# First MLP of a two-layer trunk: the relu's transpose moved from TensorE to VectorE and ScalarE, modulation loads issued two weight transfers later

## The chip, the cores and the metric

The kernel runs on one core of a Trainium2 chip. The metric is the device time of one launch in microseconds (us). A core has TensorE (PE, matrix products; PEld is its loading of the stationary operand), VectorE (DVE), ScalarE (ACT), GpSimd (POOL), and SyncE (SP), whose queue issues nearly all DMA transfers here. Each engine runs its own instructions in order and waits for the others through semaphores. SBUF is the on-chip memory of 128 partitions, PSUM the smaller one into which TensorE writes.

## What is computed

Two layers, each a token mixer and an MLP, with a modulation (adaLN) in front of each and a LayerNorm behind it. There are 256 tokens, `D_MODEL = 2048`, `D_FF = 8192`, all float32.

```python
mod = (c_act @ w_ada[i] + b_ada[i])[:, None, :]
sh_a, sc_a, g_a, sh_m, sc_m, g_m = jnp.split(mod, N_MOD, axis=-1)
h = x * (1.0 + sc_a) + sh_a
y = diff_attention(h, ...)            # layer 0; layer 1: sliding_window_attention
x = layer_norm(ALPHA * x + (1.0 + g_a) * y, ln_mix_g[i], ln_mix_b[i])
h = x * (1.0 + sc_m) + sh_m
y = jnp.square(jax.nn.relu(h @ w_up[i])) @ w_down[i]
x = layer_norm(ALPHA * x + (1.0 + g_m) * y, ln_mlp_g[i], ln_mlp_b[i])
```

## The kernel before

**Blocks, subtiles, quarters.** All weight products are cut into 89 blocks of 2048 x 512 weights (4 MB). A block is 8 subtiles n = 0 to 7 of 256 rows of weights; two subtiles are a weight quarter, one DMA transfer of 1 MB into `raw` (5 slots). For float32 accuracy each factor is split in a high and a low part: ScalarE makes `w_hi` from `raw` (`split_hi`, L528, 6 slots), VectorE makes `w_lo = raw - w_hi` in the place of `raw` (`split_lo`, L901), and TensorE does three products for each pair (hi x hi, lo x hi, hi x lo; L1709 to L1711): 12 matmuls of 128x512 for a subtile, 96 for a block. ScalarE may be at most 6 subtiles ahead of TensorE (semaphore `used`), and a weight quarter is loaded when TensorE has finished the quarter five before it (`load_raw`, L397). TensorE needs `w_lo` of subtile n before it can start subtile n.

**An MLP** is 32 blocks, in four rounds of 8: four up blocks (512 columns of `h @ w_up` each), then four down blocks that take the 2048 new features through `w_down`. While TensorE runs the next block b, the result of an up block is finished inside the others' order of work: ScalarE takes the relu out of PSUM (`up_relu`, L553, in `R`), the 256 x 512 result is transposed so that features lie on the partitions, ScalarE squares it twice (`SQ`, and rounded as `f_hi`), VectorE makes `f_lo = SQ - f_hi`. The up results are handled in block b with b % 8 = 0 to 3, where b counts the 31 blocks after the first of the MLP; blocks with b % 8 = 3 to 6 are the down blocks, and the first of them wants the last `f_lo` at its subtile 6.

**The transpose** is done in two ways. In the first MLP (layer 0) TensorE does it: 8 transposes (L1603, `turn_up`) behind its subtile 1 into the PSUM tile `turn[:, 0]`, which ScalarE squares (L560, L561, `up_square`, behind its subtile 4); VectorE's `f_lo` (L1031, `up_lo`) stands behind its subtile 4. In the second MLP (layer 1, `ON_CHIP = (1,)`) VectorE does it with 16 transposes of 32x256 (L1040), 8 behind subtile 2 and 8 behind subtile 3, each of which puts a 32-partition quarter of `R` into another 32-partition quarter of `RR`; ScalarE squares `RR` behind its subtile 5 (L572, L573).

**The modulation.** The product with `w_ada` is done on VectorE: a piece of 128x1024 (512 KB, `ada_w`, 4 slots) is multiplied by a column of `c` and added to `acc` (`ada_tile`, L929, first of 16: L926). `MLP_ADA` and `ADA_A` say behind which subtiles of a block VectorE takes a piece: in the first MLP 6 or 7 a block in blocks 0 to 27 (192 in all), in the second 32 in all. After every 16 pieces TensorE turns or sums `acc` (L1627, L1638) and VectorE takes the result (L960 and L961, or L987) behind its subtile 6. In blocks 0 to 3 of each MLP VectorE also does two passes over `x` behind subtile 7 (`affine`, L1311, L1312).

**SyncE's order** is written out by hand. `load_block` issues the four weight quarters of a block and, behind each, the pieces that VectorE takes in that quarter's subtiles. A piece (`load_ada`, L374) waits until VectorE has used the piece four before it, and everything behind it in the queue waits too.

## Time and profile before

| | |
|---|---|
| median of 3 runs | 2228.6 us (2226.92 to 2228.74) |
| the profiled execution | 2228.67 us, of which the span from first to last instruction is 2226.9 us |
| TensorE busy | 2168.5 us (97%) |
| VectorE busy | 1790.6 us (80%) |
| ScalarE busy | 981.3 us (44%) |
| bytes moved | 596.4 MB, 268 GB/s on average |
| granted TensorE clock | 0.993 on average, 1.00 in both MLPs |

The first MLP runs from 523.9 to about 1205 us, the second from 1520 to about 2195 us. The layer-0 attention with its projections stands from about 135 to 524 us. "Idle before" in a row is the time its engine stood still just before the instruction, and behind the arrow stands what it waited for. On VectorE and ScalarE an instruction's duration can be longer than the step to the next one's start, because neighbours may overlap.

### The profile page before, as it was taken

How to read it: one execution, taken by the hardware profiler on the slowest of the kernel's cores; microseconds unless marked ns; L12 is line 12 of the kernel's file. 1: busy time of each engine (PE TensorE's matmuls, PEld its weight loads, DVE VectorE, ACT ScalarE, POOL GpSimd, SP SyncE). 2: the span in 40 equal slices, each digit the busy share in tenths (PEclk: the TensorE clock that was granted, in tenths of full speed). 3: DMA queues.
4: the chain of work that ended last, by engine and by line, in shares of the span. 5: the costliest groups of instructions: out<-in, count | busy, mean ns of one | idle time of the engine just before them, and what ended most of it. 6: DMA issues, size and time to landing. Idle time of an engine off the chain costs nothing.

```text
span 2226.9 us, 26022 instructions
## 1 busy us (share of the span) xinstructions
PE 2168.5 (97%) x9952; PEld 1791.8 (80%) x9952; DVE 1790.6 (80%) x2057; ACT 981.3 (44%) x1330; POOL 33.4 (2%) x53
## 2 busy tenths in 40 slices
PE   6999999999999999999999999999999999999997
PEld 6887888877888888888888788777888888888886
DVE  6899998887997897888786888777966865874877
ACT  1135444546433443443353655536534443443441
POOL 0001000000000000000000000000000000000000
PEclk9899999999999999999999999999999999999999
DMA  9999888877999999999985643365766676666663
GB/s 360 384 331 347 322 320 300 306 245 256 361 364 325 354 366 335 325 380 350 323 311 190 198 152 119 122 207 190 236 221 223 213 241 206 219 217 219 228 234 113
DMA packets 262592, 596.41 MB, mean 268 GB/s; under 512 B 13426, under 2 KB 14788, under 8 KB 262468
## 3 DMA queue, kind: packets, MB, share of 16 engines
q1 hardware_dynamic: 254800, 579.45, 74.2%
q10 hardware_dynamic: 7668, 15.30, 2.2%
q8 instruction: 79, 1.29, 0.2%
q14 instruction: 45, 0.37, 0.0%
HBM read 592.60 MB, written 2.10 MB: 267 GB/s over the span
## 4 chain that ended last, share of the span: by engine, by line
PE 88%; DVE 7%; DMA 1%; issue 1%; ACT 1%; SPq 0%; DVEq 0%; POOL 0%; ACTq 0%; POOLq 0%
PE pair L1709 25%; PE pair L1711 25%; PE pair L1710 25%; DVE acc L916 2%; DVE w_lo L901 1%; PE pair L1967 1%; PE pair L1969 1%; PE pair L1968 1%; PE pair L1729 1%; PE pair L1731 1%; PE pair L1730 1%; PE turn L2041 1%; DMA y<-in_w_ada_dram 1%; PE turn L2022 1%; PE turn L1603 1%
## 5 line engine op out<-in xcount | busy, mean ns | idle before, releaser
L528 ACT ACTIVATE w_hi<-raw 128x1024 fp32r<-128x1024 f32 x712 | 726.8, 1056 | 620.2 <-PE pair L1711 297.4
L901 DVE TENSOR_TENSOR w_lo<-raw,w_hi 128x1024 fp32r<-128x1024 f32 x712 | 852.5, 1220 | 117.0 <-ACT w_hi L528 110.8
L1709 PE MATMUL pair<-w_hi,h_hi 128*128 128x512 f32 x1456 | 581.3, 399 | 1.5 <-DVE w_lo L901 0.8
L1711 PE MATMUL pair<-w_hi,h_lo 128*128 128x512 f32 x1456 | 567.8, 390 | 0.0
L1710 PE MATMUL pair<-w_lo,h_hi 128*128 128x512 f32 x1456 | 567.3, 390 | 0.0
L1709 PE MATMUL pair<-w_hi,f_hi 128*128 128x512 f32 x1056 | 414.0, 392 | 0.1
L1711 PE MATMUL pair<-w_hi,f_lo 128*128 128x512 f32 x1056 | 411.1, 389 | 0.0
L1710 PE MATMUL pair<-w_lo,f_hi 128*128 128x512 f32 x1056 | 410.9, 389 | 0.0
L929 DVE SCALAR_TENSOR_TENSOR acc<-ada_w,cvec,acc 128x1024 f32<-128x1024 f32 x300 | 383.6, 1279 | 1.8 <-DVE x L1312 0.9
L1709 PEld LDWEIGHTS pair<-w_hi,h_hi 128*128 128x128 f32 x1456 | 273.5, 188 | 62.9 <-DVE w_lo L901 6.3
L1711 PEld LDWEIGHTS pair<-w_hi,h_lo 128*128 128x128 f32 x1456 | 273.2, 188 | 58.4
L1710 PEld LDWEIGHTS pair<-w_lo,h_hi 128*128 128x128 f32 x1456 | 273.7, 188 | 55.5 <-issue 1.2
L1709 PEld LDWEIGHTS pair<-w_hi,f_hi 128*128 128x128 f32 x1056 | 198.2, 188 | 43.7 <-DVE w_lo L901 2.1
L1710 PEld LDWEIGHTS pair<-w_lo,f_hi 128*128 128x128 f32 x1056 | 198.3, 188 | 41.7 <-issue 1.0
L1711 PEld LDWEIGHTS pair<-w_hi,f_lo 128*128 128x128 f32 x1056 | 198.2, 188 | 41.5
L1040 DVE STREAM_TRANSPOSE work<-work 32x256 f32<-32x256 f32 x256 | 111.6, 436 | 55.7 <-ACT work L553 52.2
L553 ACT ACTIVATE work<-pair 128x1024 f32<-128x1024 f32 x32 | 32.9, 1029 | 222.3 <-PE pair L1711 222.3
L1066 DVE TENSOR_TENSOR y<-pair,y 128x1024 f32<-128x1024 f32 x30 | 36.7, 1224 | 101.2 <-PE pair L1711 101.2
L572 ACT ACTIVATE work<-work 128x1024 f32<-128x1024 f32 x16 | 17.0, 1062 | 90.7 <-DVE work L1040 90.7
L1967 PE MATMUL pair<-w_hi,f_hi 128*128 128x512 f32 x128 | 53.6, 419 | 1.9 <-DVE f_lo L1513 1.9
L1969 PE MATMUL pair<-w_hi,f_lo 128*128 128x512 f32 x128 | 50.1, 391 | 0.0
L1968 PE MATMUL pair<-w_lo,f_hi 128*128 128x512 f32 x128 | 49.9, 390 | 0.0
(190 smaller groups left out, 1669.5 us busy)
## 6 DMA issues: line engine op xcount, KB each, us to landing
ada_w<-in_w_ada_dram SPq DMA_DIRECT2D x320, 512.0 KB, 6.1
raw<-in_w_up_dram SPq DMA_DIRECT2D x128, 1024.0 KB, 6.1
raw<-in_w_down_dram SPq DMA_DIRECT2D x128, 1024.0 KB, 5.2
raw<-in_a_w_qkv_dram SPq DMA_DIRECT2D x48, 1024.0 KB, 7.6
ada_f<-in_w_ada_dram SPq DMA_DIRECT2D x44, 512.0 KB, 11.5
raw<-in_b_w_qkv_dram SPq DMA_DIRECT2D x20, 1024.0 KB, 5.2
raw<-in_a_w_o_dram SPq DMA_DIRECT2D x16, 1024.0 KB, 6.5
raw<-in_b_w_o_dram SPq DMA_DIRECT2D x16, 1024.0 KB, 5.1
```

The costliest lines, as they stand in the source:

```text
L528: act.activation(w_hi[:, (b.n * SUB + n) % SPLITS], raw[:, slot, k:k + 2], ACT.Copy).then_inc(hi_ready, 1)
L901: dve.tensor_tensor(w_lo[:, slot, k:k + 2], raw[:, slot, k:k + 2], w_hi[:, (b.n * SUB + n) % SPLITS].bitcast(F32), ALU.subtract).then_inc( ...
L916: ins = dve.scalar_tensor_tensor(dst, src, cvec[:, n % KT:n % KT + 1], dst, ALU.mult, ALU.add)
L929: ins = dve.scalar_tensor_tensor(acc[:, half], src, cvec[:, kt:kt + 1], acc[:, half], ALU.mult, ALU.add)
L1040: ins = dve.transpose(by_token(rows32(up_rows(RR), c), a), by_feature(rows32(up_rows(R), a), c))
L1066: dve.tensor_tensor(cols(y, j), pair[:, pp], cols(y, j), ALU.add).then_inc(evacuated, 1)
L1709: pe.matmul(o, hi[:, kt, at], w[:, k], start=kt == 0, stop=False)
L1710: pe.matmul(o, hi[:, kt, at], wl[:, k], start=False, stop=False)
L1711: mm = pe.matmul(o, lo[:, kt, at], w[:, k], start=False, stop=kt == KT - 1)
L1967: pe.matmul(o, f_hi[:, kt, at], w[:, k], start=kt == 0, stop=False)
L1968: pe.matmul(o, f_hi[:, kt, at], wl[:, k], start=False, stop=False)
L1969: mm = pe.matmul(o, f_lo[:, kt, at], w[:, k], start=False, stop=kt == KT - 1)
```

## The change

1. **The transpose in the first MLP** goes to VectorE and ScalarE. `turn_up` is gone from TensorE (16 x 8 transposes). VectorE does one transpose of 128x1024 behind subtile 2 (`up_turn`), which turns each 32x32 block in place of `R` into the PSUM tile `turn[:, 0]`. ScalarE then brings the blocks to their places with 16 copies of 32x256, 8 behind its subtile 3 and 8 behind its subtile 4 (`up_move`), each from one 32-partition quarter to another, and squares `RR` behind subtile 5 instead of `turn` behind subtile 4. ScalarE's relu stands behind subtile 2 instead of 1, VectorE's `f_lo` behind 5 instead of 4.
2. **The modulation pieces** are issued two weight transfers later in SyncE's order everywhere, the layer-0 attention and the second MLP included: `due` holds their counts back by `ADA_LAG = 2` quarters. Which pieces there are, their sequence, and where VectorE takes them stay as they were.

```diff
-ON_CHIP = (1,)
+ON_CHIP = (0, 1)
+BY_SCALAR = (0,)
...
+ADA_LAG = 2
...
-            def load_block(src, ada=(), ada_of=None):
+            due = deque([0] * ADA_LAG)
+
+            def load_block(src, ada=()):
                 b = st.block
                 for q in range(Q):
                     load_raw(Q * b.n + q, src(q))
-                    for n in ada:
-                        if n // 2 == q:
-                            load_ada(ada_of())
+                    due.append(sum(n // 2 == q for n in ada))
+                    for _ in range(due.popleft()):
+                        load_ada(ada_src(*next(pieces)))
                 b.n += 1
...
+            parts = [(0, 2), (0, 3), (0, 4), (1, 0), (1, 1), (1, 3), (1, 4), (0, 5), (1, 2), (1, 5)]
+            pieces = ((layer, part, half, kt) for layer, part in parts for half in range(2) for kt in range(KT))
...
+            def up_move(first, last):
+
+                def run():
+                    act.wait_ge(up_blocks, st.turned.n + 1)
+                    for i in range(first, last):
+                        a, c = i // 4, i % 4
+                        ins = act.activation(by_token(rows32(up_rows(RR), c), a),
+                                             by_feature(rows32(turn[:, 0], a), c), ACT.Copy)
+                    if last == 16:
+                        ins.then_inc(up_moved, 1)
+                return run
...
                     if layer in ON_CHIP:
+                        if i < 4 and layer in BY_SCALAR:
+                            hk[3], hk[4] = up_move(0, 8), up_move(8, 16)
                         if i < 4:
                             hk[5] = up_square_there(i)
                         block_(before=up_relu if i < 4 else None, hooks=hk, at=2)
...
+            def up_turn(b, pp):
+
+                dve.wait_ge(evacuated, b + 3)
+                dve.transpose(turn[:, 0], up_rows(R)).then_inc(up_blocks, 1)
...
                     if layer in ON_CHIP and i < 4:
-                        hooks[3] = up_turn_rest
-                        block_(before=up_turn_across, later=(5, up_rest(i)), ada=mlp_pieces(b, halves), hooks=hooks)
+                        if layer not in BY_SCALAR:
+                            hooks[3] = up_turn_rest
+                        block_(before=up_turn if layer in BY_SCALAR else up_turn_across, later=(5, up_rest(i)), ada=mlp_pieces(b, halves), hooks=hooks)
                         continue
```

ScalarE, the first two up results of the first MLP (`w_hi<-raw` is `split_hi`, `work<-pair` the relu). Before:

```order
217 L528 ACTIVATE w_hi<-raw 128x1024 x4
218 L553 ACTIVATE work<-pair 128x1024
219 L528 ACTIVATE w_hi<-raw 128x1024 x3
220 L560 ACTIVATE work<-turn 128x1024
221 L561 ACTIVATE f_hi<-turn 128x1024
222 L528 ACTIVATE w_hi<-raw 128x1024 x5
```

The same place in the changed kernel:

```order
217 L521 ACTIVATE w_hi<-raw 128x1024 x5
218 L546 ACTIVATE work<-pair 128x1024
219 L521 ACTIVATE w_hi<-raw 128x1024
220 L565 ACTIVATE work<-turn 32x2x4x32 x8
221 L521 ACTIVATE w_hi<-raw 128x1024
222 L565 ACTIVATE work<-turn 32x2x4x32 x8
223 L521 ACTIVATE w_hi<-raw 128x1024
224 L577 ACTIVATE work<-work 128x1024
225 L578 ACTIVATE f_hi<-work 128x1024
```

The splits of subtiles 4 and 5 now stand between and behind the copies, and the squares behind the split of subtile 5.

VectorE, block 1 of the first MLP (`acc<-ada_w` is a piece of modulation). Before:

```order
475 L901 TENSOR_TENSOR w_lo<-raw,w_hi 128x1024 x2
476 L929 SCALAR_TENSOR_TENSOR acc<-ada_w,cvec,acc 128x1024
477 L901 TENSOR_TENSOR w_lo<-raw,w_hi 128x1024
478 L1031 TENSOR_TENSOR f_lo<-work,f_hi 128x1024
479 L929 SCALAR_TENSOR_TENSOR acc<-ada_w,cvec,acc 128x1024
480 L901 TENSOR_TENSOR w_lo<-raw,w_hi 128x1024
```

The same place in the changed kernel:

```order
476 L908 TENSOR_TENSOR w_lo<-raw,w_hi 128x1024
477 L1046 STREAM_TRANSPOSE turn<-work 128x1024
478 L908 TENSOR_TENSOR w_lo<-raw,w_hi 128x1024
479 L936 SCALAR_TENSOR_TENSOR acc<-ada_w,cvec,acc 128x1024
480 L908 TENSOR_TENSOR w_lo<-raw,w_hi 128x1024
481 L936 SCALAR_TENSOR_TENSOR acc<-ada_w,cvec,acc 128x1024
482 L908 TENSOR_TENSOR w_lo<-raw,w_hi 128x1024
483 L1069 TENSOR_TENSOR f_lo<-work,f_hi 128x1024
```

The transpose stands between subtiles 2 and 3, `f_lo` one split and one piece later, and the number of splits and pieces is the same.

SyncE, the first blocks in which weight quarters and pieces alternate. Before:

```order
34 L374 DMA ada_w<-in_w_ada_dram 128x1024 x2
35 L397 DMA raw<-in_a_w_qkv_dram 128x4x512
36 L374 DMA ada_w<-in_w_ada_dram 128x1024 x2
37 L397 DMA raw<-in_a_w_qkv_dram 128x4x512
38 L374 DMA ada_w<-in_w_ada_dram 128x1024
```

The same place in the changed kernel:

```order
34 L377 DMA ada_w<-in_w_ada_dram 128x1024 x2
35 L400 DMA raw<-in_a_w_qkv_dram 128x4x512 x3
36 L377 DMA ada_w<-in_w_ada_dram 128x1024 x2
37 L400 DMA raw<-in_a_w_qkv_dram 128x4x512
38 L377 DMA ada_w<-in_w_ada_dram 128x1024
```

The two pieces that stood behind the first of these weight quarters stand behind the third, and so on to the end of the program.

## Rows read from the trace of the kernel before

**Rows 1.** The page: busy us, share of the span, instructions.

```profile
PE 2168.5 (97%) x9952; PEld 1791.8 (80%) x9952; DVE 1790.6 (80%) x2057; ACT 981.3 (44%) x1330; POOL 33.4 (2%) x53
```

**Rows 2.** Stages: us, then busy us (instructions) by engine, clock, DMA share, GB/s.

```profile
135.00:450.00 315.00, 313.41 (x1471) 258.20 (x1470) 288.20 (x359) 152.40 (x280) 18.74 (x32) 1.00 0.88 316
...
523.90:1205.00 681.10, 681.10 (x3094) 564.37 (x3093) 567.32 (x499) 290.20 (x293) 0.00 (x0) 1.00 0.93 334
```

**Rows 3.** Waits of SyncE's queue, 523 to 1200 us: total, times, longest.

```profile
SPq L374 <- DVE acc L929: 459.6, 176, 10.0
```

**Rows 4.** The chain that ended last, in time: start, us, what.

```profile
529.31 0.88 PE turn L1603 x8
551.97 0.87 PE turn L1603 x8
...
600.95 0.87 PE turn L1627 x8
...
1075.12 1.72 PE turn L1638 x4
```

**Rows 5.** Timeline of TensorE: start, us, instruction.

```profile
519.62 0.39 PE L1709 MATMUL pair<-w_hi,h_hi 128*128 128x512 f32 x1
...
527.78 0.39 PE L1709 MATMUL pair<-w_hi,h_hi 128*128 128x512 f32 x1
```

**Rows 6.** Timeline of ScalarE, block 1 of the first MLP.

```profile
546.55 1.03 ACT L553 ACTIVATE work<-pair 128x1024 f32<-128x1024 f32 x1 [9.66 <-PE pair L1711]
547.48 2.94 ACT L528 ACTIVATE w_hi<-raw 128x1024 fp32r<-128x1024 f32 x3
```

**Rows 7.** Timeline of VectorE, block 1 of the first MLP.

```profile
548.56 2.36 DVE L901 TENSOR_TENSOR w_lo<-raw,w_hi 128x1024 fp32r<-128x1024 f32 x2 [0.78 <-ACT w_hi L528]
550.84 1.28 DVE L929 SCALAR_TENSOR_TENSOR acc<-ada_w,cvec,acc 128x1024 f32<-128x1024 f32 x1
552.03 1.22 DVE L901 TENSOR_TENSOR w_lo<-raw,w_hi 128x1024 fp32r<-128x1024 f32 x1
554.85 1.23 DVE L1031 TENSOR_TENSOR f_lo<-work,f_hi 128x1024 fp32r<-128x1024 f32 x1 [1.60 <-ACT f_hi L561]
556.00 1.28 DVE L929 SCALAR_TENSOR_TENSOR acc<-ada_w,cvec,acc 128x1024 f32<-128x1024 f32 x1
...
562.99 1.22 DVE L1311 TENSOR_TENSOR x<-x,bc 128x1024 f32<-128x1024 f32 x1
...
565.68 1.28 DVE L929 SCALAR_TENSOR_TENSOR acc<-ada_w,cvec,acc 128x1024 f32<-128x1024 f32 x1 [0.21 <-DVE x L1312]
```

**Rows 8.** Timeline of ScalarE, layer-1 attention: small copies on half the partitions.

```profile
1268.40 0.59 ACT L603 ACTIVATE y<-pair 64x512 f32<-64x512 f32 x1 [0.93 <-PE pair L1669]
...
1269.00 0.60 ACT L603 ACTIVATE y<-pair 64x512 f32<-64x512 f32 x1
...
1302.69 0.37 ACT L860 ACTIVATE f_hi<-turn 64x256 fp32r<-64x256 f32 x1
1302.96 1.05 ACT L528 ACTIVATE w_hi<-raw 128x1024 fp32r<-128x1024 f32 x1
...
1311.60 0.38 ACT L860 ACTIVATE f_hi<-turn 64x256 fp32r<-64x256 f32 x1
1312.00 1.06 ACT L528 ACTIVATE w_hi<-raw 128x1024 fp32r<-128x1024 f32 x1
```

**Rows 9.** Timeline of VectorE, block 0 of the second MLP.

```profile
1531.87 3.58 DVE L1040 STREAM_TRANSPOSE work<-work 32x256 f32<-32x256 f32 x8 [1.61 <-ACT work L553]
```

**Rows 10.** Tile ada_w, 523 to 1200 us.

```profile
DMA to landing us min/median/max: 3.5/6.5/10.7
```

**Rows 11.** DMA issues, 135 to 450 us: count, KB each, median us to landing.

```profile
ada_w<-in_w_ada_dram SPq DMA_DIRECT2D x89, 512.0 KB, 5.4
```

**Rows 12.** Timeline of VectorE, block 5: the sum's results taken.

```profile
648.15 1.22 DVE L960 TENSOR_REDUCE mod<-turn 128x8 f32<-128x1024 f32 x1
...
649.49 1.28 DVE L929 SCALAR_TENSOR_TENSOR acc<-ada_w,cvec,acc 128x1024 f32<-128x1024 f32 x1
```

More of the change, by code:

```diff
@@ L1 @@
 import math
+from collections import deque
 from contextlib import ExitStack
@@ L407, in load_block @@
                     load_raw(Q * b.n + q, src(q))
-                    for n in ada:
-                        if n // 2 == q:
-                            load_ada(ada_of())
+                    due.append(sum(n // 2 == q for n in ada))
+                    for _ in range(due.popleft()):
+                        load_ada(ada_src(*next(pieces)))
                 b.n += 1
-            def half_stream(layer, part, half):
-                k = iter(range(KT))
-                return lambda: ada_src(layer, part, half, next(k))
-            tiles_a = iter([ada_src(0, part, half, kt) for part in (2, 3, 4) for half in range(2) for kt in range(KT)])
-            def of_a():
-                return next(tiles_a)
+            parts = [(0, 2), (0, 3), (0, 4), (1, 0), (1, 1), (1, 3), (1, 4), (0, 5), (1, 2), (1, 5)]
+            pieces = ((layer, part, half, kt) for layer, part in parts for half in range(2) for kt in range(KT))
             def load_x(j):
@@ L460, in _ @@
             for _ in FIRST_ADA:
-                load_ada(of_a())
+                load_ada(ada_src(*next(pieces)))
             st.block.n += 2
@@ L467, in _ @@
             for i in range(2, 12):
-                load_block(qkv_a(i % 3 * D + i // 3 * NC), ADA_A[PIECES_A[i]], of_a)
+                load_block(qkv_a(i % 3 * D + i // 3 * NC), ADA_A[PIECES_A[i]])
             def paired(w, i):
@@ L476, in _ @@
             for i in range(2):
-                load_block(paired(a_w_o[0], i), ADA_A[PIECES_A[12 + i]], of_a)
+                load_block(paired(a_w_o[0], i), ADA_A[PIECES_A[12 + i]])
             for j in range(2, NCH):
-                load_block(lambda q: w_rows(a_w_o[0], q * 4 * P, j * NC), ADA_A[PIECES_A[12 + j]], of_a)
+                load_block(lambda q: w_rows(a_w_o[0], q * 4 * P, j * NC), ADA_A[PIECES_A[12 + j]])
             def mlp(layer):
@@ L489, in mlp @@
                 load_block(up(0, 0))
-                parts = [(1, 0), (1, 1), (1, 3), (1, 4), (0, 5), (1, 2)] if layer == 0 else [(1, 5)]
-                tiles = iter([ada_src(l, part, half, kt) for l, part in parts for half in range(2) for kt in range(KT)])
-                def of():
-                    return next(tiles)
                 for b in range(8 * QUARTERS - 1):
@@ L498, in mlp @@
                     src = up(it, i + 1) if i < 3 else down(it, i - 3) if i < 7 else up(it + 1, 0)
-                    load_block(src, mlp_pieces(b, 2 * len(parts)), of)
+                    load_block(src, mlp_pieces(b, MLP_HALVES[layer]))
             mlp(0)
```

## The prediction

> **What bounds the kernel now.** I first read the page: TensorE is busy for 97% of the span, VectorE for 80%, ScalarE for 44% [rows 1]. The table by stages then shows where that differs. In the first MLP, the stage of the change, TensorE is busy for 681.10 of 681.10 us, so its own work sets the pace and nothing holds it up; VectorE works 567.32 of the 681.10 us (83%), ScalarE 290.20, and the DMA engines run at a share of 0.93 and 334 GB/s [rows 2]. So TensorE's work is worth its full length here, but only as long as VectorE, which has 17% left, hands over `w_lo` in time. SyncE's waits say how the loads are paced: 459.6 us of them are for VectorE to free a slot of `ada_w` [rows 3].
>
> **What TensorE gives up.** Successive turns of an up result start 551.97 - 529.31 = 22.66 us apart [rows 4]. Matmuls start 0.2267 us apart (8.16 us for 36 of them) [rows 5], so a block's 96 take 21.76 us. One turn costs 22.66 - 21.76 = 0.90 us, and 16 of them 14.4 us. That is all the change can save in this stage.
>
> **What takes its place is a chain through both other engines**, and I work it out for one block. Let T be the moment TensorE starts the block, and u the start of VectorE's transpose after T. Subtile n is wanted at T + 2.72n.
> - The earliest u. ScalarE's relu starts about 0.1 to 0.2 us after T and takes 1.03 us [rows 6] (T is 546.5: the turn at 551.97 less 24 matmuls). So u is 1.26 at the least.
> - VectorE's steps from one start to the next: a split 1.14 (two start at 548.56, the piece behind them at 550.84), a piece 1.19 to 1.20, `f_lo` 1.15, and `affine`, in the first four blocks only, 565.68 - 562.99 = 2.69 us [rows 7]. Taking a sum costs it 649.49 - 648.15 = 1.34 us [rows 12].
> - The wide transpose, 128x1024 into PSUM, is in no row. From below it is a pass of 1024 columns like the others: 1.14 us in step, 1.23 in length [rows 7]. From above it is four of the narrow ones at 3.58 / 8 = 0.45 us [rows 9], 1.8 us. I take 1.14 and 1.23, since its 1024 columns in one instruction are nearest to the rows of that width.
> - ScalarE's 16 copies of 32x256 decide. One of 64x256 takes 0.37 us. If the next may start before it ends, the step is 0.27 (1302.69 to 1302.96). But that is a copy on the first 64 partitions. A copy on the other 64 (1311.60) lets the next start only after 0.40 us, its whole 0.38 and a bit more, and two copies on different halves do not overlap either (1268.40, then 1269.00, each 0.59 to 0.60 long) [rows 8]. VectorE's narrow transposes with the same access patterns, each to another quarter than the last, also come at 0.45 us a piece [rows 9]. All 16 copies change their quarter from one to the next, so I take 0.39, with 0.28 and 0.40 as ends. ScalarE's wide instructions come every 0.94 us and last 1.06 [rows 6].
>
> The Trainium skill speaks against my value: "ScalarE: Activation LUTs", section "What ACT_TABLE_LOAD costs", says that back-to-back ACTIVATEs overlap by about 93 ns and that one takes 186 ns + 0.833 ns an element, which would make a step of 399 - 93 = 306 ns. No row with changing partitions shows that overlap; by it alone the result would be an estimated 2235 us.
>
> Laid out from u with 0.39: the transpose ends at 1.23, copies 1 to 8 run from 1.26 to 4.38, split_hi(4) ends at 5.44, copies 9 to 16 run to 8.57, split_hi(5) ends at 9.63, the second square at 11.51. VectorE meanwhile does split 3 and its piece (to 3.48) and then waits: split 4 at 5.47 (2.0 us idle), split 5 at 9.66 (1.85 idle), `f_lo` at 11.54 (0.7 idle). Before, the idle time of such a block was 0.78 + 1.60 [rows 7]; now it is 4.6 us, and none of it shrinks when VectorE is late, because the chain starts with VectorE's own transpose. From `f_lo` on: piece 5, split 6 (ready at u + 15.11), split 7 and the next block's splits 0 to 2 with four pieces among them; the next transpose can start at u + 24.39. TensorE turns a block over in 21.76. So each up block falls 2.63 us behind, while before the change the same engines had 22.66 us for less work. Split 6 is wanted at 16.33, which allows u = 1.22: there is no slack at all, not even when all begins in time. I therefore expect TensorE to stand still for `w_lo`, at subtile 6 first.
>
> **The sum over the 16 blocks.** In rounds 2 to 4 the four down blocks before cost VectorE 8 x 1.14 + 7 x 1.19 + 1.14 = 18.6 us each against 21.76, so it comes to the first up block in time. Round 2: 0.04 + 2.63 + 2.63 + 3.06 (one sum costs VectorE 1.34 and TensorE 0.90 [rows 4, 12]) = 8.4. Round 3: the same less one first piece (L926, 0.54 us shorter) = 7.8. Round 4: 6.8, since its sum costs TensorE 1.72 us [rows 4] and VectorE 1.15, and it too has a first piece. Round 1: `affine` adds 2.69 to VectorE's cycle, 27.08 against 21.76, so 5.32 us a block: 2.1 + 5.3 + 5.3 + 5.8 = 18.5. Together 41.5 us of new idle time on TensorE, against 14.4 saved: +27.1 us. Everything not named costs nothing on the path: relu behind subtile 2 instead of 1 (ScalarE waited 9.66 us there [rows 6]), ScalarE's total of about 8 x 0.94 + 0.93 + 6.2 + 1.9 = 16.6 us of 24.4, and the last `f_lo` of a round, ready at u + 12.8 where TensorE wants it at 16.3.
>
> **The later modulation pieces.** A piece for quarter k was issued as soon as a slot was free; four slots are 4 / 6.86 of a block or 12.7 us. Now it is issued behind the transfer for k + 2, when TensorE starts k - 2, 10.9 us before k. It lands 6.5 us later in the median and 10.7 at most [rows 10], behind about 2 us of issue, so 2.4 us before TensorE's start of k, or 1.8 us after it at worst. VectorE must have it 0.3 us after that start or earlier to be in time with the next split. In the first MLP that holds in the median, and in the new up blocks VectorE comes later still. The weight transfers, no longer behind 459.6 us of waits [rows 3], come earlier, which helps ScalarE and not TensorE. In the attention TensorE takes results for which VectorE must be some 4.5 us ahead (its step `combine` stands behind the split two subtiles on); a piece lands after 5.4 us there [rows 11], which leaves about 1 us. DMA demand doesn't rise, since the blocks get longer. I put +1 us for the whole, between -1 and +15.
>
> So 2228.67 + 27.1 + 1.0 = **2256.8 us**. The profiled execution's own time, 2228.67, stands at the median of the runs, 2228.6, so nothing is added for that.
>
> **The rivals.**
> 1. The copies overlap (0.28 us each). Then split_hi(4) and (5) come 0.9 and 1.8 us earlier, the cycle is 22.57, an up block falls 0.81 us behind, rounds 2 to 4 lose 1.1 + 1.1 + 0.1, and round 1 loses 0.3 + 3.5 + 3.5 + 3.9 = 11.2. 13.5 lost and 14.4 saved: 2227.8 us, no change. It decides at a copy step of about 0.29. For it speaks the 0.27 of the first half's copies, against it both other pairs [rows 8] and the transposes [rows 9].
> 2. VectorE keeps up altogether, and the 14.4 us are kept: 2214.3 us, faster. It needs a cycle of at most 21.76, that is copies at 0.22 us and no idle left. VectorE's 17% of free time [rows 2] speaks for it, but that time lies in the down blocks, and round 1 alone, 27.08 us by the rows, is hard to argue away.
> 3. Pieces come late. If landing is near 10.7 us more often, VectorE waits at even subtiles, about half of the 16 units of the attention cost 1 to 2 us each, and first up blocks start 1 to 2 us late: +8 to +20 on the forecast, 2265 to 2277.
> 4. The wide transpose writes PSUM at the pace of the narrow ones (1.8 us): 0.6 us more in each of 13.5 full cycles, +8: 2265.
>
> **How the numbers follow.** The chain as worked out has 0.55; rival 1, with steps between 0.28 and 0.31 (up to 2236), 0.17; rival 2 0.05; rival 3 0.13; rival 4 0.10. The range takes in rival 1 below and rivals 3 and 4 above: 2227 to 2274 us. About 4.5 us (0.2%) is what a measurement of this kernel can tell from no change. Slower than 2233: 0.82. Within 0.2%: 0.11. Faster: 0.07.
>
> **What the profile would show.** Right: PE gone from 100% in the first MLP, waits of TensorE for `w_lo` of some 40 us, longest in its first 100 us, with stalls at subtile 6 and at subtile 0 behind `affine`; eight copies in 3.1 us; VectorE waiting for `w_hi` about 2 us twice in each of 16 blocks; up blocks 24.4 us apart, 27.1 in round 1; the second MLP unchanged. Wrong: eight copies in 2.3 us (rival 1); VectorE waiting for DMA of `ada_w` before TensorE stalls, in the attention too (rival 3); a wide transpose over 1.3 us (rival 4). A first MLP still at 100% busy would make the whole argument wrong.

## The result and the profile after

The changed kernel takes **2276.9 us** in the median of four runs (2276.6 to 2278.4), the kernel before 2228.7 beside it (2226.9 to 2229.1): a ratio of 1.0219 with a 95% interval of 1.0202 to 1.0237. It is 48.2 us slower. I had forecast 2256.8, in a range of 2227 to 2274: the sign was right, and the time lies 3 us above the range. Two runs far above all others, one of the kernel before (5884.0 us) and one of e12 below (4435.9 us), stand in no median.

The page of the changed kernel (as in [rows 1]), and its group for the copies (their number, busy us, mean ns of one, idle time before them):

```profile
PE 2172.7 (96%) x9824; PEld 1779.4 (78%) x9824; DVE 1810.9 (80%) x2073; ACT 1082.5 (48%) x1586; POOL 34.9 (2%) x53
...
L565 ACT ACTIVATE work<-turn 32x256 f32<-32x256 f32 x256 | 96.3, 376 | 50.9 <-DVE turn L1046 47.9
```

The stages of it (as in [rows 2]; the first MLP now runs from 535.8 to about 1249.5 us; a short window is added that I come to below):

```profile
135.00:450.00 315.00, 307.49 (x1424) 252.40 (x1423) 279.09 (x349) 145.87 (x272) 20.21 (x32) 0.98 0.84 302
535.80:1249.50 713.70, 676.88 (x2953) 546.67 (x2952) 585.31 (x512) 388.55 (x546) 0.00 (x0) 1.00 0.89 319
390.00:392.00 2.00, 2.00 (x7) 1.61 (x6) 0.35 (x2) 1.54 (x2) 0.00 (x0) 0.50 0.00 0
```

In [rows 2] TensorE was busy for all of the first MLP. Now it stands for 37 us of it, and it stands in the attention too, where the kernel's code for TensorE, VectorE and ScalarE is the same as before.

Blocks are numbered through the program; block 17 is the second block of the first MLP, in which the first up result is finished. From the start of each block's first matmul in TensorE's timelines (the program's first two blocks scatter by some 3 us from one profiled run to the next, with the lag or without, so the stretch behind them has a row of its own):

| us | before | change | turning alone (e1) | lag alone (e2) |
|---|---|---|---|---|
| start of block 17 | 523.7 | 535.8 | 522.1 | 535.8 |
| blocks 2 to 16 (the attention) | 382.9 | 395.0 | 382.9 | 396.8 |
| four up results, round 1 | 91.6 | 106.9 | 106.9 | 94.1 |
| round 2 | 91.6 | 98.9 | 96.5 | 91.6 |
| round 3 | 92.5 | 98.2 | 96.9 | 92.5 |
| round 4 | 92.5 | 97.9 | 96.1 | 92.5 |
| blocks 17 to 46 | 678.2 | 713.7 | 708.1 | 680.7 |

So 12.1 us were lost before the first MLP and 35.5 in it; the second MLP takes what it took. TensorE and VectorE wait in the changed kernel from 524 to 1250 us (total, times, longest):

```profile
DVE w_lo L908 <- ACT w_hi L521: 64.3, 34, 3.0
PEld pair L1722 <- DVE w_lo L908: 53.1, 39, 2.8
ACT work L565 <- DVE turn L1046: 47.9, 16, 5.4
PE pair L1722 <- DVE w_lo L908: 36.5, 34, 2.4
DVE acc L936 <- DMA ada_w<-in_w_ada_dram: 33.8, 25, 3.0
```

The last row is new in kind: before the change VectorE never waited for a piece. In the attention, 160 to 524 us, the same view has it as well, which is the sign that the prediction had named for its rival 3. With it come waits of TensorE for VectorE:

```profile
DVE acc L936 <- DMA ada_w<-in_w_ada_dram: 29.5, 18, 4.2
...
PE turn L1695 <- DVE mod L956: 3.2, 1, 3.2
...
PE turn L1695 <- DVE gate L979: 1.8, 1, 1.8
PE turn L1920 <- DVE y L1435: 1.8, 1, 1.8
```

The kernel before has one of the three there, and shorter:

```profile
PE turn L1682 <- DVE gate L972: 0.9, 1, 0.9
```

SyncE's queue shows what the lag does. In the first MLP of the kernel before its waits were for VectorE (459.6 us [rows 3]), and for TensorE only (523 to 1200 us):

```profile
SPq L397 <- PE pair L1711: 76.0, 26, 5.1
```

In the changed kernel (524 to 1250 us) the queue mostly waits for TensorE before a weight transfer (L400), with the pieces behind it, and less for VectorE before a piece (L377):

```profile
SPq L400 <- PE pair L1724: 455.2, 109, 6.6
SPq L377 <- DVE acc L936: 123.7, 58, 6.3
```

The turned up result itself looks as it was worked out. VectorE's timeline of the fourth one (as [rows 7]):

```profile
618.46 1.25 DVE L1046 STREAM_TRANSPOSE turn<-work 128x1024 f32<-128x1024 f32 x1
619.62 1.20 DVE L908 TENSOR_TENSOR w_lo<-raw,w_hi 128x1024 fp32r<-128x1024 f32 x1
...
623.92 1.22 DVE L908 TENSOR_TENSOR w_lo<-raw,w_hi 128x1024 fp32r<-128x1024 f32 x1 [1.92 <-ACT w_hi L521]
...
628.14 1.23 DVE L908 TENSOR_TENSOR w_lo<-raw,w_hi 128x1024 fp32r<-128x1024 f32 x1 [1.79 <-ACT w_hi L521]
630.03 1.22 DVE L1069 TENSOR_TENSOR f_lo<-work,f_hi 128x1024 fp32r<-128x1024 f32 x1 [0.67 <-ACT f_hi L578]
```

ScalarE's timeline beside it (as [rows 6]):

```profile
619.75 3.07 ACT L565 ACTIVATE work<-turn 32x256 f32<-32x256 f32 x8 [5.42 <-DVE turn L1046]
622.83 1.06 ACT L521 ACTIVATE w_hi<-raw 128x1024 fp32r<-128x1024 f32 x1
623.91 3.11 ACT L565 ACTIVATE work<-turn 32x256 f32<-32x256 f32 x8
```

VectorE's three waits are 1.92, 1.79 and 0.67 us (2.0, 1.85 and 0.7 in the prediction); eight copies take 3.07 us, a step of (3.07 - 0.38) / 7 = 0.385 (0.39).

### The profile page after: what moved, and what is told of

Read it like the earlier page. It is cut to its first block, busy times and chain, and to the rows that moved or that the text cites. A ratio compares the mean times of both kernels' runs of the same rounds, so it can differ in the third digit from the quotient of the medians.

```text
span 2274.8 us, 26022 instructions
## 1 busy us (share of the span) xinstructions
PE 2172.7 (96%) x9824; PEld 1779.4 (78%) x9824; DVE 1810.9 (80%) x2073; ACT 1082.5 (48%) x1586; POOL 34.9 (2%) x53
## 4 chain that ended last, share of the span: by engine, by line
PE 68%; DVE 15%; issue 6%; ACT 6%; DMA 4%; SPq 0%; POOL 0%; ACTq 0%; DVEq 0%; POOLq 0%
PE pair L1722 19%; PE pair L1724 18%; PE pair L1723 18%; DVE acc L936 4%; ACT work L565 3%; DVE w_lo L908 3%; DMA ada_w<-in_w_ada_dram 3%; DVE acc L923 2%; PE pair L1980 1%; PE pair L1982 1%; PE pair L1981 1%; ACT w_hi L521 1%; PE pair L1742 1%; DVE turn L1046 1%; PE turn L2054 1%
## 5 line engine op out<-in xcount | busy, mean ns | idle before, releaser
L1723 PE MATMUL pair<-w_lo,f_hi 128*128 128x512 f32 x1056 | 411.7, 390 | 0.0
L565 ACT ACTIVATE work<-turn 32x256 f32<-32x256 f32 x256 | 96.3, 376 | 50.9 <-DVE turn L1046 47.9
L577 ACT ACTIVATE work<-work 128x1024 f32<-128x1024 f32 x32 | 33.7, 1052 | 90.7 <-DVE work L1052 90.7
```

The source lines that it names most:

```text
L565: ins = act.activation(by_token(rows32(up_rows(RR), c), a), by_feature(rows32(turn[:, 0], a), c), ACT.Copy)
L1723: pe.matmul(o, hi[:, kt, at], wl[:, k], start=False, stop=False)
```

## The experiments

Every kernel was timed beside the kernel before (2227.6 to 2227.9 us). Differences are to that.

### Which part costs what: e1, e2, e3, e11

e1 is the change without the lag, e3 (`ADA_LAG = 1`) with one transfer of it.

```diff
-ADA_LAG = 2
+ADA_LAG = 0
```

> The transpose on VectorE and ScalarE alone, with the modulation pieces back in their old places in SyncE's order. Theory (two separate costs: the chain VectorE - ScalarE - VectorE in the up blocks as forecast, +27 us, and late pieces, +12 us in the attention and about 8 us in the first MLP because VectorE comes late to the first up block of a round): 2228.7 + 27 = about 2256 us, with the attention stage back to its old length and the up blocks 24.4 us apart. Rival (the whole excess in the first MLP, 35.5 us, comes from the chain, and pieces have no part in it): 2264 us. Second rival (the late issue was a help in the first MLP, since the weight transfers came earlier): above 2264 us, with ScalarE waiting for the weights.

> The changed kernel with pieces one weight transfer later instead of two. Theory: a piece then lands about 5.4 us earlier against TensorE, VectorE's lead is capped near 8 us instead of 3, so that both attention stalls (3.2 and 3.6 us) and the late start of the rounds go: about 2256 us, like no lag at all. Rival (the cost grows in proportion to the lag): half of the lag's 20 us is left, about 2266 us.

e2 is the lag alone, with TensorE turning:

```diff
-ON_CHIP = (0, 1)
-BY_SCALAR = (0,)
+ON_CHIP = (1,)
+BY_SCALAR = ()
```

> TensorE turns the relu as before; only the pieces are issued two weight transfers later. Theory: the attention stage is 12 us longer as in the changed kernel, the first MLP hardly (VectorE's lead over TensorE is capped at 2 to 3 us, but nothing there needs more): about 2241 us. Rival (the +12 us in the attention come with the change as a whole and not with the late pieces): 2229 us. Rival 2 (a capped lead costs in the first MLP as well, 5 us or more): 2246 us or above.

**Measured.** e1 2258.1 us (2257.2 to 2259.8), ratio 1.0136 [1.0121, 1.0152]: +30.2. e2 2243.3 us (2242.3 to 2246.4), 1.0072 [1.0057, 1.0087]: +15.4, of which 13.9 in blocks 2 to 16 of its profiled run. e3 2257.9 us, 1.0136: one transfer of lag costs nothing. The two parts add up to 45.6 of the 48.2 us. The turning is what the prediction had it to be (27.1), the lag is not (1). The first MLP's waits of e1 in the same view as above show the chain with no piece late:

```profile
ACT w_hi L521 <- DMA raw<-in_w_down_dram: 130.4, 37, 6.6
...
DVE w_lo L908 <- ACT w_hi L521: 71.3, 44, 3.0
PEld pair L1722 <- DVE w_lo L908: 47.4, 37, 2.8
```

e11 is the change with the lag from the first MLP on:

```diff
-            due = deque([0] * ADA_LAG)
+            due = deque()
...
+            due.extend([0] * ADA_LAG)
             mlp(0)
```

> The change, but the two transfers of lag begin with the first MLP; the layer-0 attention is served as before the change. The attention was 12.1 us longer in the change and not at all with the turning alone. Theory: that part belongs to the lag wholly, so the attention takes its old time and the whole is 2276.9 - 12.1 = 2265 us, with the first MLP at about 713 us as in the change. Rival 1: the lag costs nothing in the MLP itself, and its rounds were slow there only as the attention left VectorE behind: 2258 us, as without lag. Rival 2: the attention's loss moves to the beginning of the MLP: 2270 us or more.

**Measured** 2262.4 us (2261.8 to 2264.0), 1.0158 [1.0143, 1.0173]. Block 17 starts at 523.3, and blocks 17 to 46 take 713.8 us, as in the change and 5.7 more than in e1. So the lag has two prices that add up: by the profiled runs 12.1 us in the attention and 5.7 in the MLP, by the medians 14.5 (2276.9 - 2262.4) and 4.3 (2262.4 - 2258.1). The sum in the MLP is the change's, its parts are not quite: rounds 2 to 4 take 98.0, 99.6 and 99.2 us, and the down blocks behind round 1 take 89.0 instead of 90.6.

### The chain of the turning: e4, e5, e10

e4 is e1 with half of the copies left out, so half of each up result isn't put in its place.

```diff
-                    for i in range(first, last):
+                    for i in range(first, last, 2):
```

> As the transpose alone with the old order of pieces, but only 8 of the 16 copies of each up result are made (the other half of the rows is left out, so the result isn't the reference's). Theory (the copies stand on the chain, 0.38 us each without overlap): the cycle of an up block shrinks by 8 x 0.38 = 3.0 us to about 21.4, under TensorE's 21.76, in rounds 2 to 4, and in round 1 to about 24.0, of which 2.3 us a block remain: 2228.7 - 14.4 + about 9 = 2223 us. Rival (what holds VectorE is its own amount of work, not the wait for ScalarE): within 5 us of the kernel with all copies, about 2251 us or more.

**Measured** 2220.6 us (2219.4 to 2221.9), 0.9966 [0.9955, 0.9978]: 37.4 us less than e1 for 8 fewer copies in each of 16 blocks. The copies' time carries through the chain to TensorE, and TensorE's own saving shows once the chain is short.

e5 is e1 with 16 copies, but each stays in its partition quarter and four in a row have the same one (the blocks don't reach their places).

```diff
-                        a, c = i // 4, i % 4
-                        ins = act.activation(by_token(rows32(up_rows(RR), c), a),
-                                             by_feature(rows32(turn[:, 0], a), c), ACT.Copy)
+                        ins = act.activation(by_token(rows32(up_rows(RR), i // 4), i % 4),
+                                             by_feature(rows32(turn[:, 0], i // 4), i % 4), ACT.Copy)
```

> As the transpose alone with the old order of pieces, but each of the 16 copies stays in its own 32-partition quarter (four in a row on quarter 0, four on 1, and so on; the blocks don't reach their places, so the result isn't the reference's). Theory A (copies don't overlap because neighbours work on different quarters): 12 of the 16 then start 0.28 us after the one before, the copies take 4.9 instead of 6.1 us, and the kernel about 1.1 x 13.5 = 15 us less than 2258, so 2243. Theory B (an instruction that starts above partition 0 never lets the next one overlap): only the copies of quarter 0 gain, 0.3 us, about 2254 us. Theory C (a copy of 32 partitions never overlaps): 2258 us.

e10 (made from e7, below) exchanges the loops, `a, c = i % 4, i // 4`: the quarter written stays for four copies, the one read changes.

> The kernel of e7 with the two loops of the 16 copies exchanged: four copies in a row now write the same partition quarter and read another one each, where before four in a row read the same quarter and wrote another each. The same 16 copies. It asks which side's change of quarter prevents the overlap of ScalarE's neighbouring copies. If the output side decides, three of four steps fall to 0.27 to 0.28 us, a batch of 16 takes about 5 us instead of 6.1, and the time falls by 1 to 3 us below e7's 2222.3. If the input side decides (or either does), the steps stay at 0.38 to 0.39 us and the time is e7's within 2 us.

**Measured.** e5 2234.9 us (2234.4 to 2236.4), 1.0034 [1.0021, 1.0048], 23 us less than e1. e10 2225.5 us (2221.1 to 2230.9), 0.9992 [0.9982, 1.0001]: 3.2 us above e7's median, within the scatter of the two. ScalarE's timeline of e5, one batch of eight:

```profile
762.61 2.36 ACT L564 ACTIVATE work<-turn 32x256 f32<-32x256 f32 x8 [1.43 <-DVE turn L1045]
```

The same timeline of e10, all sixteen:

```profile
547.13 6.19 ACT L565 ACTIVATE work<-turn 32x256 f32<-32x256 f32 x16 [0.38 <-DVE turn L1046]
```

In e5 the step is (2.36 - 0.37) / 7 = 0.28 us on average. Taken one by one it is 0.27 between copies of the same quarter, whichever quarter that is, and 0.375 where the next quarter begins. In e10 it is (6.19 - 0.38) / 15 = 0.387, as in the change. In the change four copies in a row read the same quarter and write another each, in e10 they write the same and read another each: neighbouring copies overlap only where neither the quarter read nor the quarter written changes. e5 gained more than the 15 us I expected, since I had taken 1.1 us for 13.5 blocks. A batch of eight is 3.07 - 2.36 = 0.71 us shorter, so a block's two are 1.42 us shorter, and all 16 blocks gain it: 22.7 us. In its profiled run each of the four rounds is 5.4 to 5.8 us shorter than in e1, 1.4 us a block.

### What the order could have given: e6, e7, e9, e8

e6 is e1 with the transposing moved back in ScalarE's order, so that the splits VectorE needs meanwhile are made before the copies: the relu behind subtile 4, all 16 copies behind 5, the squares and `f_lo` behind 6. e7 adds to it that `affine` of the first MLP is done in blocks 4 to 7 instead of 0 to 3 (the third pair of lines below), and e9 does that alone to e1. ScalarE's `load_affine`, the load that `affine` needs, moves along in e7 and e9 and stands a subtile later in e6 and e7; that line isn't shown.

```diff
-                            hk[3], hk[4] = up_move(0, 8), up_move(8, 16)
+                            hk[5] = up_move(0, 16)
...
-                            hk[5] = up_square_there(i)
-                        block_(before=up_relu if i < 4 else None, hooks=hk, at=2)
+                            hk[6 if layer in BY_SCALAR else 5] = up_square_there(i)
+                        block_(before=up_relu if i < 4 else None, hooks=hk, at=4 if layer in BY_SCALAR else 2)
...
-                    if b < NCH:
-                        hooks[7] = affine(site, b)
+                    if b - 4 * (layer in BY_SCALAR) in range(NCH):
+                        hooks[7] = affine(site, b - 4 * (layer in BY_SCALAR))
...
-                        block_(before=up_turn if layer in BY_SCALAR else up_turn_across, later=(5, up_rest(i)), ada=mlp_pieces(b, halves), hooks=hooks)
+                        block_(before=up_turn if layer in BY_SCALAR else up_turn_across, later=(6 if layer in BY_SCALAR else 5, up_rest(i)), ada=mlp_pieces(b, halves), hooks=hooks)
```

> The transpose on VectorE and ScalarE with old order of pieces, but another order on ScalarE: relu behind the split of subtile 4, all 16 copies behind 5, squares behind 6; VectorE's f_lo behind 6. Theory (the loss is VectorE's waiting for splits that stand behind copies): VectorE's idle time a block falls from 4.6 to about 0.5 us, its cycle to 20.3 us, TensorE never stalls in rounds 2 to 4, and in round 1 (23.0 us with the passes over x) about 5 us in all: 2228 - 14.4 + 5 = 2219 us, faster than before. Rival (VectorE's amount of work, which the order doesn't change, is the bound): about 2255 us. Rival 2 (the weights for subtiles 4 and 5 aren't there so early): ScalarE waits for DMA, and the time is between 2225 and 2245.

> As the reordered kernel, and the passes over x of the first MLP stand in blocks 4 to 7 instead of 0 to 3. Theory: they fall in down blocks, where VectorE has 3.1 us to spare and they take 2.7, so round 1 stalls no more either: 2228 - 14.4 = 2214 us. Rival (VectorE's lead, used up in blocks 4 to 7, is missing at the start of round 2): 2219 us, no better than without the move.

> The transpose alone in the order of the change with old order of pieces, only the passes over x moved to blocks 4 to 7. Theory: round 1 then loses what the others lose, about 8.2 us instead of 18.5: 2258 - 10.3 = 2248 us. Rival (the stalls of round 1 are due to the start of the MLP, not to these passes): 2258 us.

**Measured.** e6 2230.8 us (2228.3 to 2236.3), 1.0016 [1.0006, 1.0025]; e7 2222.3 us (2219.3 to 2227.9), 0.998 [0.997, 0.9989]; e9 2247.4 us (2247.2 to 2248.0), 1.009 [1.0072, 1.0108]. The order is worth 27 us, `affine`'s place 10.6 without it and 8.5 with it. e6 and e7 came out 12 and 8 us above what I expected; e6 lies where its second rival had it, with ScalarE waiting for the weights. In the profiled runs e7 won 8.1 us in round 1 over e6 and lost 3.9 in round 2, though in its last two up blocks and not at its start, where e7's rival had put it. What was left in e7 was the weights: SyncE still stood behind pieces (469.0 us), and ScalarE for `raw`. e8 is e7 with one transfer of lag, `ADA_LAG = 1`.

> The kernel of e7 (later copies, affine in blocks 4 to 7), but with the modulation pieces issued one weight transfer later. In e7 TensorE still waited for w_lo when VectorE's lead had run out, and VectorE had waited for w_hi before. Theory: the pieces' waits in SyncE's queue hold the weights back, and one transfer of lag frees them without making a piece late (e3 and e1 were alike, 2257.9 and 2258.1 us): ScalarE's waits for raw fall, VectorE's waits for w_hi fall a little, and the time is 2219 to 2222 us. Rival: the weights were early enough in e7; then the time is e7's 2222 us within 2 us, as for e1 and e3. Second rival: with the lead small, one transfer of lag already makes pieces late in this order: 2226 us or more, with waits of VectorE for ada_w.

**Measured** 2213.2 us (2212.1 to 2214.2), 0.9936 [0.9921, 0.9951]: 14.5 us faster than the kernel before, the fastest of all, and 6 below the least that I expected. Waits for weights and pieces in the first MLP of e7 (the last row is SyncE's queue's own):

```profile
ACT w_hi L521 <- DMA raw<-in_w_down_dram: 131.5, 44, 5.2
ACT w_hi L521 <- DMA raw<-in_w_up_dram: 114.5, 37, 6.2
...
SPq L377 <- DVE acc L936: 469.0, 176, 9.1
```

The same waits of e8:

```profile
ACT w_hi L521 <- DMA raw<-in_w_up_dram: 25.2, 11, 5.1
...
ACT w_hi L521 <- DMA raw<-in_w_down_dram: 5.0, 2, 3.2
DVE acc L936 <- DMA ada_w<-in_w_ada_dram: 2.5, 3, 1.0
...
SPq L377 <- DVE acc L936: 208.6, 101, 4.6
```

The first MLP of e8 as a window (as in [rows 2]):

```profile
523.40:1187.00 663.60, 663.60 (x2953) 548.78 (x2952) 584.03 (x512) 389.14 (x544) 0.00 (x0) 1.00 0.95 342
```

663.6 us against 678.2 before the change: TensorE is busy throughout again, and 14.6 us are saved, the 16 turns at 0.90 of the prediction. One transfer of lag frees the weights (246 us of waits become 30) and leaves VectorE 2.5 us of waits for pieces. In e3 the same lag freed them too (ScalarE's waits for `raw` fell from 233 to 50 us), and gained nothing, as the copies and not the weights set the pace there.

### The lag: e12, e13, e14, e15

In the attention TensorE's half turns (L1695, behind its subtiles 2 and 3) write a PSUM tile that VectorE must have emptied; the steps that empty it, the first sum's gates (`gate_part`, L979) and two modulation outputs (`mod_out`, L956), stand behind VectorE's subtiles 5 and 6. So VectorE has to be 3 to 4 subtiles (8 to 11 us) ahead. TensorE's timeline of the kernel before in block 11 shows how little was to spare:

```profile
381.25 0.60 PE L1682 MATMUL turn<-ident,work 128*128 128x128 f32 x4
```

VectorE's timeline of it has the step that TensorE waits for, done at 381.00, 0.25 us before:

```profile
380.84 0.16 DVE L949 TENSOR_TENSOR mod<-turn,bvec 128x8 f32<-128x8 f32 x1
```

In block 4 the gates came 0.87 us too late before the change already, and `y`, for which TensorE waits just ahead of them, was done 1.07 us in time.

TensorE's timeline of the changed kernel in block 11:

```profile
389.16 1.08 PE L1695 MATMUL turn<-ident,work 128*128 128x128 f32 x4 [3.20 <-DVE mod L956]
389.90 0.77 PE L1722 MATMUL pair<-w_hi,h_hi 128*128 128x512 f32 x1
390.47 0.63 PE L1723 MATMUL pair<-w_lo,h_hi 128*128 128x512 f32 x1
390.90 0.63 PE L1724 MATMUL pair<-w_hi,h_lo 128*128 128x512 f32 x1
```

VectorE's there, with a piece that came late and the step that TensorE waits for:

```profile
377.13 1.29 DVE L936 SCALAR_TENSOR_TENSOR acc<-ada_w,cvec,acc 128x1024 f32<-128x1024 f32 x1 [1.49 <-DMA ada_w<-in_w_ada_dram]
...
388.85 0.16 DVE L956 TENSOR_TENSOR mod<-turn,bvec 128x8 f32<-128x8 f32 x1
```

Against the start of block 11 (371.24 before, 375.79 in the change) the step is 3.46 us later. The wait of 1.49 us above and one of 1.82 at 370.89, both for a piece, are 3.31 of them.

e12 is e2 with these results taken earlier; e13 has only the second of the two lines.

```diff
-            sums = {4: {5: gate_part(0, 0)}, 5: {0: gate_part(0, 1)}, 6: {5: gate_part(1, 0)}, 7: {0: gate_part(1, 1)},
-                    9: {6: mod_out(0, 3, 2, 0, at=0)}, 11: {6: mod_out(0, 3, 2, 1, at=0)},
+            sums = {4: {2: gate_part(0, 0)}, 5: {0: gate_part(0, 1)}, 6: {5: gate_part(1, 0)}, 7: {0: gate_part(1, 1)},
+                    9: {3: mod_out(0, 3, 2, 0, at=0)}, 11: {3: mod_out(0, 3, 2, 1, at=0)},
```

> The lag of two alone, with TensorE turning as before the change (e2, 2243.3 us, 15.4 over before), but in the attention VectorE takes the first sum's gates behind its subtile 2 of block 4 instead of 5, and the two modulation outputs behind subtile 3 of blocks 9 and 11 instead of 6. Theory: the attention's loss comes from three turning steps of TensorE (behind its subtiles 2 and 3) that wait for VectorE to have taken these results, which stood 3 to 4 subtiles ahead in VectorE's order and so wanted a lead that the late pieces no longer leave. With the results taken earlier these stalls (1.8, 3.2 us and the like) and the low granted clock behind them go: 7 to 12 us back, 2232 to 2236 us. Rival: any of VectorE's steps there comes late, whatever its place, and the loss only moves to the waits for w_lo: 2241 us or more.

> As e12 (the lag of two alone), but only the modulation outputs of blocks 9 and 11 are taken behind subtile 3; the gates of block 4 stay behind subtile 5. In e12 block 11 went back from 31.9 to 25.8 us, while block 4 grew from 36.1 to 40.2, as VectorE stood 8.8 us before the gates. Theory: the two places are independent, so the gain of block 11 stands alone: 2243.3 - 6 = 2237 us. Rival: block 11's loss was a matter of luck in how the pieces landed, and without e12's delay in block 4 it returns: 2243 us.

e14 is e13 with the lag from block 6 on.

```diff
-            due = deque([0] * ADA_LAG)
+            due = deque()
...
             for i in range(2, 12):
+                if i == 6:
+                    due.extend([0] * ADA_LAG)
```

> As e13, and the lag of two begins only with the transfers of block 6. Block 4's pieces are issued as before the change. Theory: VectorE's wait of 4.4 us for a piece of block 4, behind which TensorE stood 3.5 us for y and 0.8 for the gates, was the other half of the attention's loss. The attention then takes its old time, and what is left of the lag is its cost in the MLP, about 3 us: 2230 to 2232 us. Rival: any late piece in this stage costs TensorE something wherever it lies, and the loss moves to blocks 6 to 10: 2235 us or more.

**Measured.** e12 2242.7 us (2241.8 to 2245.7), 1.0072 [1.0055, 1.0089]: no gain, so my theory fell as I had put it. Block by block it splits: block 11 takes 25.8 us (31.9 in e2, 25.8 before), block 4 takes 40.1 (36.1 in e2, 29.8 before), since VectorE now stands in front of the gates. VectorE's timeline of e12:

```profile
195.74 0.69 DVE L979 SCALAR_TENSOR_TENSOR gate<-turn,bc 128x512 f32<-128x512 f32 x1 [8.80 <-PE turn L1663]
```

TensorE's timeline of e12, behind it:

```profile
206.84 0.47 PE L1920 MATMUL turn<-ident,y 128*128 128x128 f32 x1 [8.44 <-DVE y L1435]
```

In e2 the first loss in block 4 was a late piece at the same point of VectorE's order, and again `y`. VectorE's timeline of e2:

```profile
190.59 1.28 DVE L936 SCALAR_TENSOR_TENSOR acc<-ada_w,cvec,acc 128x1024 f32<-128x1024 f32 x1 [4.41 <-DMA ada_w<-in_w_ada_dram]
```

TensorE's timeline of e2:

```profile
201.08 0.48 PE L1920 MATMUL turn<-ident,y 128*128 128x128 f32 x1 [3.53 <-DVE y L1435]
```

e13 2240.1 us (2236.6 to 2242.2), 1.0052 [1.0037, 1.0067]: 3 us below e2 in the median, with block 11 at 25.8 us again. e14 2233.2 us (2228.8 to 2236.0), 1.0022 [1.0013, 1.0032], with blocks 4 and 11 at 29.8 and 25.8. e14 came out between its theory (2232 at most) and its rival (2235 at least). So the attention's loss lay in these two places: of e2's 13.9 us, 2.1 are left, 1.6 of them in its last five blocks, and 4.9 us are lost in the MLP (2.5 in e2). In block 4 it is `y` and not the gates that cost the time: TensorE's wait for the gates in e2, 0.84 us, is no longer than before the change. e13's median fell by less than the 6 us of block 11, with runs 5.6 us apart. Its profiled run fell by 4.6: 6.0 in block 11 and 0.7 in block 4, less 0.8 in the program's first two blocks, 0.4 in the attention's last five and 1.0 in the MLP.

e15 is e8 with two transfers of lag, `ADA_LAG = 2`.

> The kernel of e8 (2213.2 us) with two transfers of lag in place of one: so the change itself, with the copies, squares and f_lo later and affine in blocks 4 to 7. Theory: the attention loses its 12 us again, as it has the same order as in the change, and the first MLP, where VectorE now has a lead, waits for late pieces only at a few places: 2213 + 12 + 0 to 5 = 2225 to 2230 us. Rival: with two transfers of lag the pieces come too late in the MLP whatever the order, as in the change (713.8 us with the lag against 708.1 without), and cost it 6 us or more: 2231 us or more.

**Measured** 2233.2 us (2230.0 to 2235.3), 1.0022 [1.0012, 1.0032]: 20 us above e8, block 17 at 536.2, and blocks 17 to 46 in 670.0 us instead of 663.6. The rival held in its number: the second transfer of lag costs about 12 us in the attention and 6 in the MLP in either order. The place in the MLP is another, though: 5.5 of the 6.4 us lie in blocks 23 and 24 (25.6 and 24.4 us, in e8 21.8 and 22.7), two of the down blocks in which `affine` now stands, and the up blocks lose almost nothing.

## Why the prediction was wrong in size

**The turning, +27.1 forecast, +30.2 measured (e1).** Step by step:
- TensorE's saving, 14.4 us: right. It is hidden in the change and shows in e8 (14.6).
- The copy step, 0.39 between 0.28 and 0.40: 0.385. Right, and for the reason given (the quarter changes); e10 adds that the side read is enough.
- The wide transpose, 1.23 long and 1.14 in step: 1.25 and 1.16. Right, so rival 4 is out.
- The cycle of 24.39 us: up blocks 24.4, 24.4, 25.4 and 24.8 us apart in round 2 of the change, where the third holds a sum. In round 1 of the change 27.1, 27.1 and 28.8 after the first. Right.
- Rounds 2, 3 and 4 of e1: 4.9, 4.4 and 3.6 us over the kernel before, where the sum gives 8.4, 7.8 and 6.8 less 3.6 each = 4.8, 4.2 and 3.2. Right.
- Round 1 of e1: 15.3 against 18.5 - 3.6 = 14.9. Right. Another 1.7 us lie in the down blocks right behind it, where the granted clock is 0.90 from 628 to 645 us (in the changed kernel 0.94 from 644 to 674). These 1.7 us, and 1.1 by which the rounds lie above the sum, are what the profiled run's 29.9 has over the forecast.
- TensorE's waits for `w_lo`, "some 40 us" with stalls at subtile 6 and at subtile 0 behind `affine`: 36.5 in the change, 31.9 in e1. Right, but they begin a subtile earlier, at subtile 5.

**The lag, +1 forecast, +15.4 alone and 18.8 on top of e1.** I had put it between -1 and +15. This is the step that failed, at the words "that holds in the median" and "which leaves about 1 us". My figures for a piece were near enough: issued 10.9 us before TensorE's start of its quarter, 2 us of issue and 6.5 to land, so there 2.4 us before that start. Paired one by one in the trace, the pieces of the first MLP land 3.5 us before it at the median and 1.9 us behind it at worst (8.1 and 2.7 us before it in the kernel before), those of the attention 5.7 us before it (13.9), so for `combine`, 4.5 us ahead, the forecast's 1 us was there. But I compared a piece's arrival only with the moment at which VectorE must have it to keep TensorE fed, 0.3 us after that start. What the lag does is tie a piece to TensorE's progress, and with that it caps how far ahead VectorE can be: in the down blocks of the first MLP its lead (from the end of a split to TensorE's start of that subtile) was mostly 3 to 6 us in the change, before it mostly 5 to 8.9. Two things in this kernel live on a larger lead.
- The attention's steps that VectorE must have done 3 to 4 subtiles ahead. I had looked for them and named only `combine`, at 4.5 us. The ones that bind were the output behind subtile 6 in block 11, with 0.25 us to spare before the change, and `y` in block 4, with 1.07: two places, not eight of 16 units, and 4 to 6 us each, not 1 to 2 (e13, e14).
- The rounds. In e1 the first up block of round 2 takes 22.1 us, because VectorE comes to it with 7.7 us of lead and spends it; in the change 24.4, since it has 1.3 there (from the two engines' timelines, at subtile 1). So rounds 2 to 4 lose 2.4, 1.2 and 1.9 us more than in e1, 5.6 in the MLP (5.7 in e11).

Rival 3 had this case, "8 to 20 on the forecast, 2265 to 2277", and the time is at its upper end. I gave it 0.13 and cut the range at 2274, below its end. Its mechanism was right in what is late, and in the MLP also in where it is paid: its first up blocks that "start 1 to 2 us late" are those of rounds 2 to 4. In the attention it was wrong, and that two places of 4 to 6 us cost about what eight units at 1 to 2 us would have is luck.

**Rival 1**, the overlapping copies, fell with the step of 0.385. The Trainium skill's 93 ns of overlap between back-to-back ACTIVATEs ("ScalarE: Activation LUTs", "What ACT_TABLE_LOAD costs") is there where the partitions stay: in e5 a copy takes 0.366 us and the next starts 0.272 after it, an overlap of 0.094. Where they change it is not, and the measured step decides. **Rival 2** needed another order (e8), not a luckier one. No noticeable part of the 48.2 us is left without a place (47.9 between the profiled runs): 12.1 in the attention, 35.5 in the first MLP, of which e1 has 29.9 and the lag 5.7.

## What to carry to other kernels

Ask of a delayed load not only whether it comes in time, but how much lead its consumer may still build: a transfer whose issue is tied to the slower engine's progress caps the lead of the faster one, and every step that stands ahead in the faster engine's order is paid from that lead. Work handed to a helper engine in the middle of a block belongs behind the inputs that the others need meanwhile: the same instructions cost +30 us in one order and, with `affine` moved and one transfer of lag, gave back 14.5 in another. A parameter that does nothing in one order (one transfer of lag, e3) can be worth 9 us in the next (e8), so it is to be tried again after each.

## What the hardware did that I had not expected

- **A stall costs more than its length.** In block 11 TensorE stood 3.20 us (from 385.96), and then its matmuls came 0.427 us apart instead of 0.227 for about 5 us (389.9 to 394.7); the granted clock is 0.50, the 1.2 GHz level, from 388.0 to 394.9 us, and 1.00 before and behind. Twelve matmuls at 0.427 instead of 0.227 are 2.4 us on top. The same follows the stalls of 1.78 and 1.82 us in block 4 (clock 0.50 from 205 to 207 us, where it is 1.00 in the kernel before).
- **Overlap hangs on the partitions.** ScalarE's neighbouring 32x256 copies start 0.27 us apart in the same quarter, 0.375 to 0.39 when the quarter read or written changes. Over the 32 batches of eight in the first MLP e5's order is worth 22.7 us of ScalarE's time, and 23 us of the kernel's.
